# Two-block transformer kernel: the first two tiles of a layer are multiplied together, and its first loads and convolution taps are reordered

## The reference, cut to what matters

```python
for l in range(DEPTH):                       # DEPTH = 2
    h = rmsnorm(x, norm_mix[l])
    proj = jnp.einsum('btd,de->bte', h, w_in[l])
    q, k, v, u, ug, ga, gb = jnp.split(proj, SPLITS, axis=-1)
    ...
    a_out = sliding_window_attention(q, k, v, sinks[l])
    c_out = conformer_conv(u, ug, ...)        # a = u * sigmoid(ug), 31 taps per channel over time
    ...
```

## Time and profile before

| | |
|---|---|
| three runs | 2151.68, 2152.4, 2152.4 us (median 2152.4) |
| the profiled execution, its own time | 2152.17 us |
| its span from first to last instruction | 2150.4 us |
| busy PE, PEld, DVE, ACT, POOL | 2140.1, 1853.9, 1577.9, 1035.5, 115.9 us |
| the chain that ended last | PE 93%, DVE 3%, ACT 3% |
| HBM read | 235.76 MB, 111 GB/s over the span |

### The profile page before, as it was taken

The page is one execution under the profiler, slowest core; times in us unless marked ns, Lnnn a source line. Parts: engine busy times, 40 slices in busy tenths (PEclk is TensorE's granted clock), DMA queues, the critical chain, the costliest instruction groups (busy, mean ns, idle before and its releaser), DMA issues.

```text
span 2150.4 us, 31580 instructions
## 1 busy us (share of the span) xinstructions
PE 2140.1 (100%) x12112; PEld 1853.9 (86%) x12112; DVE 1577.9 (73%) x2438; ACT 1035.5 (48%) x1707; POOL 115.9 (5%) x177
## 2 busy tenths in 40 slices
PE   9999999999999999999999999999999999999998
PEld 6888889999888888889999888888888899888887
DVE  8999888888546999888888544664766568888723
ACT  5678555555323678555555323332555344222312
POOL 0000001111000000001110000000000000000000
PEclk9999999999999999999999999999999999999999
DMA  5212246665223221246665323223232331222222
GB/s 181 80 67 79 79 121 188 177 193 154 95 100 130 69 79 66 87 124 181 184 187 149 108 91 143 98 79 128 96 93 80 101 119 60 98 98 98 94 95 76
DMA packets 60428, 243.11 MB, mean 113 GB/s; under 512 B 7264, under 2 KB 7776, under 8 KB 44960
## 3 DMA queue, kind: packets, MB, share of 16 engines
q1 hardware_dynamic: 47216, 217.97, 29.3%
q0 software_dynamic: 12672, 23.07, 6.4%
q10 hardware_dynamic: 432, 0.64, 0.1%
HBM read 235.76 MB, written 2.10 MB: 111 GB/s over the span
## 4 chain that ended last, share of the span: by engine, by line
PE 93%; DVE 3%; ACT 3%; DMA 0%; issue 0%; SPq 0%; DVEq 0%
PE mm L2297 22%; PE mm L2299 22%; PE mm L2298 22%; PE sp L2299 7%; PE sp L2297 7%; PE sp L2298 7%; DVE conv_y L1462 1%; PE ob L2523 1%; ACT probs L705 1%; DVE probs L1492 1%; PE sp L2495 1%; ACT probs L713 1%; PE sp L2510 0%; DVE w_lo L1361 0%; DMA x<-in_x_dram 0%; PE ob L2297 0%
## 5 line engine op out<-in xcount | busy, mean ns | idle before, releaser
L2297 PE MATMUL mm<-in_hi,w_hi 128*128 128x512 f32 (+1 forms) x1520 | 538.4, 354 | 2.3 <-DVE in_lo L1395 1.7
L2299 PE MATMUL mm<-in_hi,w_lo 128*128 128x512 f32 (+1 forms) x1520 | 531.7, 350 | 0.0
L2298 PE MATMUL mm<-in_lo,w_hi 128*128 128x512 f32 (+1 forms) x1520 | 531.7, 350 | 0.0
L646 ACT ACTIVATE w_hi<-w_raw 128x2048 fp32r<-128x2048 f32 (+3 forms) x145 | 256.2, 1767 | 455.8 <-PE mm L2299 337.3
L1361 DVE TENSOR_TENSOR w_lo<-w_raw,w_hi 128x2048 fp32r<-128x2048 f32 (+3 forms) x149 | 323.2, 2171 | 196.6 <-ACT w_hi L646 195.3
L2297 PEld LDWEIGHTS mm<-in_hi,w_hi 128*128 128x128 f32 x1520 | 285.5, 188 | 46.3 <-issue 6.8
L2299 PEld LDWEIGHTS mm<-in_hi,w_lo 128*128 128x128 f32 x1520 | 285.5, 188 | 38.1
L2298 PEld LDWEIGHTS mm<-in_lo,w_hi 128*128 128x128 f32 x1520 | 285.7, 188 | 36.9 <-issue 1.0
L1462 DVE SCALAR_TENSOR_TENSOR conv_y<-conv_in,parl,conv_y 128x512 f32<-128x512 f32 x240 | 169.5, 746 | 1.3
L2297 PE MATMUL sp<-in_hi,w_hi 128*128 128x512 f32 (+1 forms) x432 | 146.3, 339 | 0.0
L2299 PE MATMUL sp<-in_hi,w_lo 128*128 128x512 f32 (+1 forms) x432 | 145.8, 337 | 0.0
(11 more groups left out here) (496 smaller groups left out, 4432.8 us busy)
## 6 DMA issues: line engine op xcount, KB each, us to landing
w_raw<-in_w_dram SPq DMA_DIRECT2D x120, 1024.0 KB, 4.8
w_raw<-in_w_dram SPq DMA_DIRECT2D x85, 512.0 KB, 4.3
w_raw<-in_w_dram SPq DMA_DIRECT2D x32, 704.0 KB, 3.8
w_raw<-in_w_dram POOLq DMA_DIRECT2D x44, 256.0 KB, 3.6
w_third_sum<-in_w_dram SPq DMA_DIRECT2D x44, 256.0 KB, 4.9
w_third_sum<-in_w_dram POOLq DMA_DIRECT2D x44, 256.0 KB, 3.6
out_dram<-z_rows SPq DMA_DIRECT2D x8, 256.0 KB, 2.0
rope<-in_rope_dram SPq DMA_DIRECT2D x3, 512.0 KB, 3.4
```

The lines of the kernel that those rows point to most:

```text
L646: e.activation(whi[:, slot, 0:cols], raw[:, slot, 0:cols], ACT.Copy).then_inc(s_whi, whi_out.up())
L2297: MM(out, ah, bh, start=first, stop=False, **kw)
L2298: MM(out, ah, bl, start=False, stop=False, **kw)
L2299: return MM(out, al, bh, start=False, stop=last, **kw)
```

## The change

- **Pair.** `first_pair` multiplies u0 (bank 0) and ug0 (bank 2) together, k by k: 6 matmuls for each k instead of 3. The sum of squares comes 18 matmuls later than before: after 6 of the 8 steps of tile u1, which now goes to bank 1. Tile ug1 goes to bank 3, and the four transposes come behind it. The host lays out chunk 0 so that a quarter of it holds two steps k of both tiles.
- **Loads.** SP loads x tile by tile with the quarters of chunk 0 between, then chunk 1 as two quarters and a half. ACT issues the first quarter of chunk 0 and then the eight parameter columns that scale the input; the other 208 come by SP behind chunk 1. ACT and DVE split the weights quarter by quarter in that order.
- **Takes.** DVE takes bank 0 and bank 2, gates, takes banks 1 and 3 at once, and then works on taps.
- **Taps.** TAPS_U loses two taps before the low part of chunk 3 and two before the last take of chunk 5; each of the heads 4 to 7 gets one more. This holds in both layers.
- **Zeros.** WARM is 5 products of 256 columns instead of 4 of 512.

```diff
-TAPS_U, TAPS_KV = ((4, 6), (3,), (2, 3, 1), (2, 4)), (1, 1)
-TAPS_Q = ((2, 0, 4, 2), (2, 2, 3, 3)) + 2 * ((2, 2, 3, 3),) + (QT - 4) * ((2, 2, 2, 3),)
+TAPS_U, TAPS_KV = ((2, 6), (3,), (2, 3, 1), (2, 2)), (1, 1)
+TAPS_Q = ((2, 0, 4, 2),) + (QT - 1) * ((2, 2, 3, 3),)
-WARM = 4
+WARM = 5
@@ SP @@
-            x_tiles(4, 6, s_xk[3])
-            first_weights(slice(CH // 2, CH), s_rest)
-            x_tiles(6, KT, s_xk[4])
-            load(1, 1)
+            first_weights(0, quarters[2], s_w0[1])
+            x_tiles(4, 5, s_xk[3])
...
+            first_weights(1, quarters[1], s_w1[1])
+            first_weights(1, slice(CH // 2, CH), s_raw[1])
+            w_free.skip(1)
+            e.dma_start(pars[:, KT:], PARS[:, KT:]).then_inc(s_cst, 16)
@@ ACT @@
-            e.dma_start(pars[:], PARS[:]).then_inc(s_x0, 16)
-            for cs, told in ((slice(0, CH // 4), s_raw[0]), (slice(CH // 4, CH // 2), s_more)):
-                e.dma_start(raw[:, 0, cs], W[0:1, :, cs].rearrange("a p c -> (a p) c")).then_inc(told, 16)
+            e.dma_start(raw[:, 0, quarters[0]], W[0:1, :, quarters[0]].rearrange("a p c -> (a p) c")).then_inc(s_raw[0], 16)
+            e.dma_start(pars[:, 0:KT], PARS[:, 0:KT]).then_inc(s_x0, 16)
@@ DVE @@
                 take(tA[:, 0:T], 0)
-                take(tB[:, 0:T], 1)
+                take(tB[:, 0:T], 2)
                 prep(0, CH // 2)
                 up_gate(0)
+                take(tA[:, 0:T], 1)
+                take(tB[:, 0:T], 3)
                 convolve(TAPS_U[0][0])
-                take(tA[:, 0:T], 2)
+                prep(1, CH // 2)
...
+                up_gate(1)
                 convolve(TAPS_U[0][1])
-                take(tB[:, 0:T], 3)
-                prep(1, CH // 2)
-                up_gate(1)
                 convolve(TAPS_U[1][0])
@@ PE @@
-                for d in range(2):
-                    e.wait_ge(s_w, w_in.next())
-                    out_tile(d, 0, KT * d, xh, xl, KT, None if d else inp)
+                e.wait_ge(s_mmf, taken.next())
+                for k in range(KT):
+                    if k % HK == 0:
+                        e.wait_ge(s_w, w_in.next())
+                    e.wait_ge(s_in, inp.next())
+                    for d in range(2):
+                        a = slice((2 * k + d) * P, (2 * k + d + 1) * P)
+                        ins = mm3(four[2 * d], whi[:, 0, a], wlo[:, 0, a], xh[:, k, :], xl[:, k, :],
+                                  k == 0, k == KT - 1)
...
+                product(1, 1, 0, xh, xl, range(KT - 2), last=False)
                 e.wait_ge(s_one, 1)
                 sum_halves(0, ssr[:])
...
-            for _ in range(WARM):
-                MM(mi[:], tD[:, 0:P], tD[:], start=True, stop=True)
+                MM(mi[:, 0:TH], tD[:, 0:P], tD[:, 0:TH], start=True, stop=True)
```

More of the change, by code:

```diff
@@ L357, in program @@
         OP = CH // 4
+        quarters = tuple(slice(i * OP, (i + 1) * OP) for i in range(4))
         A12, A22, A21, A11 = (slice(i * OP, (i + 1) * OP) for i in range(4))
@@ L752, in _ @@
             first_hi((1,))
[L753 removed]
+            e.wait_ge(s_w0[0], 16)
+            prep_part(0, quarters[1])
             e.wait_ge(s_xk[1], 16)
             first_hi((2,))
[L756 to L757 removed]
             e.wait_ge(s_xk[2], 16)
             first_hi((3,))
+            first_square((0,))
+            e.wait_ge(s_w0[1], 16)
+            prep_part(0, quarters[2])
             e.wait_ge(s_xk[3], 16)
[L761 to L762 removed]
+            first_hi((4,))
+            first_square((1,))
             e.wait_ge(s_xk[4], 16)
[L764 to L767, removed]
+            first_hi((5,))
+            e.wait_ge(s_w0[2], 16)
+            prep_part(0, quarters[3])
+            first_square((2,))
+            e.wait_ge(s_xk[5], 16)
+            first_hi((6,))
+            e.wait_ge(s_xk[6], 16)
+            first_hi((7,))
+            e.wait_ge(s_w1[0], 16)
+            prep_part(1, quarters[0])
+            e.wait_ge(s_w1[1], 16)
+            prep_part(1, quarters[1])
+            first_square(range(3, KT))
             added.skip(KT)
[L769 removed]
+            e.wait_ge(s_raw[1], raws[1].next(16))
+            prep_part(1, slice(CH // 2, CH))
             sum_hi()
@@ L1424, in add_first @@
                 return TT(dst, ga[:, 0, :], ga[:, k, :], ALU.add)
-            add_first(1).then_inc(s_do, own.up())
[L1427 to L1433, removed]
+            e.wait_ge(s_x0, 32)
+            first_lo((0,))
+            first_part(0, quarters[0]).then_inc(s_w, w_out.up())
+            first_lo((1,))
+            first_part(0, quarters[1]).then_inc(s_do, own.up())
+            e.wait_ge(s_do, own.now())
+            first_lo((2, 3))
+            first_part(0, quarters[2]).then_inc(s_w, w_out.up())
+            first_lo((4,))
+            add_first(1).then_inc(s_do, own.up())
+            first_lo((5,))
+            first_part(0, quarters[3]).then_inc(s_do, own.up())
             add_first(2).then_inc(s_do, own.up())
             first_lo((6, 7))
-            prep(0, CH, CH // 2)
+            first_part(1, quarters[0]).then_inc(s_do, own.up())
+            e.wait_ge(s_do, own.now())
+            first_part(1, quarters[1]).then_inc(s_w, w_out.up())
             for k in range(3, KT - 1):
@@ L1440, in _ @@
             e.sem_inc(s_sum, KT - 1)
-            prep_and_sum()
+            first_part(1, quarters[2]).then_inc(s_do, own.up())
+            lo(ssr[:], ssum[:], sumh[:], rot)
+            e.wait_ge(s_do, own.now())
+            TT(wlo[:, 1, quarters[3]], raw[:, 1, quarters[3]], r32(whi[:, 1, quarters[3]]),
+               ALU.subtract).then_inc(s_w, w_out.up())
             first = sum(TAPS_U[0])
@@ L2343, in first_pair @@
             def first_pair():
-                for d in range(2):
-                    e.wait_ge(s_w, w_in.next())
-                    out_tile(d, 0, KT * d, xh, xl, KT, None if d else inp)
+                e.wait_ge(s_mmf, taken.next())
[7 more added lines that the diff above has]
+                                  k == 0, k == KT - 1)
+                        if k == KT - 1:
+                            ins.then_inc(s_mm, tiles.up())
+                e.wait_ge(s_w, w_in.next())
+                e.wait_ge(s_mmf, taken.next())
+                product(1, 1, 0, xh, xl, range(KT - 2), last=False)
                 e.wait_ge(s_one, 1)
                 sum_halves(0, ssr[:])
-                for d in range(2):
-                    e.wait_ge(s_w, w_in.next())
-                    product(2 + d, 1, KT * d, xh, xl, range(KT)).then_inc(s_mm, tiles.up())
-                    if d == 0:
-                        e.wait_ge(s_cst, 16)
-                        e.wait_ge(s_msf, misc_taken.now(-1))
-                        by_tokens(ems)
-                taken.skip(2)
+                product(1, 1, KT - 2, xh, xl, range(KT - 2, KT), first=False).then_inc(s_mm, tiles.up())
+                e.wait_ge(s_w, w_in.next())
+                product(3, 1, KT, xh, xl, range(KT)).then_inc(s_mm, tiles.up())
+                e.wait_ge(s_cst, 32)
+                e.wait_ge(s_msf, misc_taken.now(-1))
+                by_tokens(ems)
             def pair(hi_, lo_, ready=None, norm=False):
```

38 lines of the change are left out of this document (23 added, 15 removed).

## The result

| | before | after |
|---|---|---|
| median | 2152.06 us (7 runs, 2151.68 to 2152.4) | 2160.27 us (7 runs, 2158.12 to 2161.68) |
| ratio, 95% interval | | 1.0037 [1.0027, 1.0047] |
| the profiled execution | 2152.17 us, span 2150.4 | 2161.68 us, span 2159.9 |

The changed kernel is 0.4% slower, by 8.2 us in the medians and 9.5 us in the profiled executions. The forecast was 2154.1, and its range ended at 2157.4: it was wrong, by more than the range allowed. The changed kernel also scatters over 3.6 us, the kernel before over 0.7.

A forecast was written before the change was run, and what follows sets the result against it. PE was taken as the bound, waiting at chunk 4 for DVE's chain behind a later sum of squares. Layer 0's -1.1 and layer 1's +2.8 gave +1.7 us, so 2154.1, range 2149.8 to 2157.4.

The forecast's parts named there:

- The first product, 7.05, bounds 6.0 to 8.0: Front of layer 0: PE starts its first product at 7.05, 1.0 us earlier than before.
- The walk: Front, followed k by k through loads, DVE and PE: only k = 6 late, by 0.15 us; pair ends near 18.2.
- The second rival: Front: loads land as late as now, pair starts at 8.0, sum at 24.0; 2155.3 us in all; chance 13%.
- The zeros ... end at 5.5: no bound any more: Program start: the zeros cost 4.1 us instead of 6.51, end at 5.5 and no longer hold the first product.
- From the sum to chunk 4, 21.2 us: Both layers: DVE's chain lets PE start chunk 4 21.2 us after the sum of squares.
- The pause of 2.8 us: Ahead of chunk 4, each layer: PE's own work takes 18.4 us after the sum, so it waits 2.8 us for DVE.
- Layer 1, +2.8: Layer 1: the sum comes 4.1 us later, so chunk 4 starts 2.8 us later; bounds 0 to 3.6.
- Layer 0, 1.1 earlier: Layer 0: chunk 4 starts at 44.0 against 45.13, 1.1 us earlier; bounds 2.6 earlier to 0.1 later.
- The clock behind the pauses: PE behind its waits at chunk 4: the forecast's sum included no cost for a lower clock.
- The third rival: PE's clock falls in the pause at chunk 4, at most 3.3 us each: 2157.4 or 2160.7 us; chance 13%.
- The heads: Heads 4 to 7, both layers: the added tap of about 0.66 us fits q's 0.76 of slack, costing 0.
- First rival: Chunk 4: PE meets no pause and the front's gain is kept; 2148.3 us, or 2150.3 with half; chance 14%.

The follow-up runs named there:

- e5: The changed kernel with ACT's first two issues swapped, the eight columns ahead of the first quarter of weights: 2158.21 us, ratio 1.0029.
- e1: The changed kernel with 8 products of zeros at the start instead of 5: 2157.35 us, ratio 1.0026.
- e9: The changed kernel with 8 products of zeros and 12 useless matmuls ahead of PE's wait for chunk 4: 2155.86 us, ratio 1.0019.
- e8: The kernel of e7 with the eight columns issued ahead of the first quarter and 7 products of zeros: 2151.09 us, ratio 0.9996.
- e6: The changed kernel with both tap tables of the kernel before: 2163.31 us, ratio 1.0053.
- e3: The kernel before with only the sum of squares moved 18 matmuls later and the transposes behind tile ug1: 2159.83 us, ratio 1.0035.
- e2: The changed kernel with 12 useless matmuls ahead of PE's wait for chunk 4, in both layers: 2157.47 us, ratio 1.0025.
- e4: The changed kernel with four more taps moved from ahead of chunk 4's low part to before chunk 5's last take: 2152.93 us, ratio 1.0005.
- e7: The changed kernel with 8 zeros, first taps ahead of bank 3's take or moved later, extra taps only in heads 5 and 7: 2151.89 us, ratio 0.9999.
- e10: The kernel of e8 with the extra taps of heads 5 and 7 moved behind the heads: 2151.04 us, ratio 0.9997.

## Why the prediction was wrong

**The first product, 7.05, bounds 6.0 to 8.0: missed at 8.36.** The walk took x's first tile, the quarter and the columns as one sum of 0.53 MB. The rows of after show two things that the sum hides. The columns, issued second on ACT's queue, landed behind the quarter, so `in_hi` could not start before 6.04; and the quarter itself landed near 5.9 even with the columns ahead of it (e5). That it shares the engines with x1 and the next quarter is a likely reason; no run shows it. The second rival had the late start, 8.0, with 13%; its sum at 24.0 would have been 23.5 with the clock up (e1, e9).

**"The zeros ... end at 5.5: no bound any more": the step that failed.** I priced the zeros as a load on PE that had become shorter. They were also what raised PE's clock before the first product. With five eighths of the columns they end at 6.05 (the sum had 5.5), PE idles 2.3 us, and the next 5.6 us of the program run at half pace. So the sum came at 26.27, outside its bounds of 21.3 to 24.0: these held DVE and the loads, and took PE at 0.23 a matmul. The operand was on time (`sum_lo` 22.69 against 22.5), and that by luck: DVE's line began at 6.88 instead of 5.6 and took 15.8 us instead of 16.9. PE was not on time. e1 gives 2.8 us back with three more zeros, but its sum at 23.45 still waits for no operand (`sum_lo` is ready at 22.47 there): it is PE's work from a first product at 8.13. e8, which starts at 7.54, has it at 22.98.

The column of the granted clock misled here. It says 1.00 for the front of the changed kernel too:

```profile
9.00:12.00 3.00, 3.00 (x9) 2.32 (x8) 2.96 (x5) 3.00 (x7) 0.00 (x0) 1.00 1.06 397
```

In this window the matmuls follow each other at 0.43. The first record of the clock in this trace stands at 13.96 (in the kernel before at 7.10), and ahead of it the column shows 1.00 all the same. The starts of the matmuls tell it. So of the earlier trace rows only what lies behind 7.10 spoke of the clock.

**From the sum to chunk 4, 21.2 us: right,** 21.24 in both layers, with its parts: taps -1.50 (1.58 by e6), the new wait for tile ug1 0.5 (0.47). The pause of 2.8 us was 3.02 and 3.04. Layer 1, +2.8: right, 2.82. Layer 0, 1.1 earlier: 2.4 later, all of it from the sum; with the clock up it is 0.3 earlier (e9), and 1.1 would have needed the sum at 22.8 as well.

**The clock behind the pauses, which the sum put at nothing: the other step that failed.** The third rival, 13%, is what happened, in both pauses of the profiled execution. Its mechanism was named and its price bounded at 3.3 us a pause; it measured 1.7. What was wrong is its chance, and that the sum held no part of it. Against it I set that the clock had held through the front's pauses; but in those PE idled 0.89 us and less, and in the new ones it was to stand for 2.8. The rows that I had said nothing of pauses between these and the end of the program, so they could not speak against it. The forecast of 2154.1 with two such falls is 2157.5, with the front's 2.8 and the heads' 1 it is 2161.3. The profiled execution, with all of them, has 2161.68; the median is 2160.27. That the runs between 2158.12 and 2161.68 differ by the falls in them is likely, as e9 without a fall scatters over 0.75 us; they were not profiled.

**The heads, "0, bounds 0 to 0.1 each in the tightest of four": too small.** They cost 0.5 us in each layer, 0.9 to 1.1 in sum. The sum of 0.66 against 0.76 of slack in q held to 0.05 us. But q is not the only thing that DVE makes there: `q_scale` stands behind the same tap, ACT's work up to the probabilities hangs on it without a pause, and PE waited for those (0.16 us at 181.38). I had read one consumer of two. The other wait (0.20 us, at 147.27) is in a head without an added tap; with the old tables it is gone too (e6).

**First rival (no pause): wrong in both layers,** as is the whole idea that the front's gain could pass the sum. DVE's chain from the sum sets chunk 4; e3, which moves only the sum and the transposes, loses nearly as much as the full change.

The Trainium skill (TensorE: Matmul & The Clock Gate, HAM oscillation — how this bites in real kernels) describes a product loop whose waits for loads throttle PE again each time, and counts the price of a throttled stretch as half of its length. The trace agrees: 3.41 us at 0.50 cost 1.7, and e9, without a fall, is 1.5 us under e1's profiled run with one.

## What to carry to other kernels

When a change makes TensorE wait in one long piece, price the wait and then what follows it: here 3 us of pause cost 4.7 where the clock fell. Filler work in front of the first product also keeps the clock up: when you shorten it, look at the gap that it leaves up to the product (here it cost 2.8 us). And a dependency that is moved back in a hardware loop over layers costs in every layer, while the loads it is meant to meet exist only in the first.

## What the runs showed of the hardware

- PE's clock fell behind five of six pauses of 3.0 us (both of the changed kernel, both of e5, one of two of e1), behind one of two of 2.27 (e3), both of 4.6 (e6), and behind none of 1.3 us or less (all from start to start). A fall was granted for 3.41 us, once for 6.83. It mostly set in after PE had begun again, up to 1.5 us after (e1), but 0.1 us before it in e5 and 2.1 before it in e6. Whether it comes is not fixed by the program: pauses of 3.02 and 3.05 in one execution ended differently.
- The same holds between the zeros and the first product: with five zeros and 2.4 to 3.2 us from the last one's start to the first product, the clock was low to 13.96 (the changed kernel), fell at 7.9 for 3.41 us (e2, e4, e5), or rose at 6.6 and stayed (e6). With seven or eight zeros, and 1.9 us or less in between, it was up within 0.1 us of the first product's start each time (e1, e7, e8, e9, e10).
- The kernels with such a place scatter more, mostly: 3.6 us the changed kernel, 5.0 e5, 2.9 e2, 2.8 e4 (at the front alone), 2.2 e6, 1.9 e1 and 1.3 e3. Without one it was 0.75 to 1.3 (e7 to e10), and 1.2 to 1.4 for the kernel before in the rounds of the experiments.
- A load of 4 KB issued 0.43 us behind one of 256 KB on the same queue landed 0.6 us behind it, 4.8 us after its issue. Issued first, the same 4 KB landed after 2.7 us (e5), and the 108 KB of the kernel before after 2.6.
